# A ring of six raw weight units in the expert passes, and a router in another order with eight gather banks

## Chip, cores and metric
One core of one Trainium2 chip runs the whole program. The metric is device time in microseconds, the median of the runs.

## What is computed
Two layers over 256 tokens of width 1024. In each: a mixing block (RMSNorm, one combined projection, four mixers, gated branch products, an output projection), then a mixture of experts with a two-level choice:

```python
h = rmsnorm(x, norm2_g[l])
g_logits = t @ w_group + b_group              # 4 groups, the best one is taken
e_in = expert logits (t @ w_expert + b_expert) of that group   # 4 experts, the best 2
hid = silu(t @ w_e_gate) * (t @ w_e_up)        # experts 1024 -> 256
out = sum over the 2 experts of weight * (hid @ w_e_down)      # 256 -> 1024
x = x + out
```

## The kernel before
**Weights.** All large products are made of float32r pieces: a number is split into hi and lo, and each product is three matmuls (hi hi, hi lo, lo hi; lines 1309 to 1311). Weights come from HBM in units of up to 128 x 2048 float32 (1 MB), each by two DMAs that the SyncE queue issues in the order of use (`load`). A unit lands in a raw slot; ScalarE copies it to `w_hi` (`hi`, L500), VectorE makes `w_lo` by a subtraction (`lo`, L777). Raw slots and split slots are rings of four: a load into a slot waits until `lo` of the unit four before it is done; `hi` waits until TensorE has used the unit four before.

**Stages of a layer.** The mixing block takes 36 units. The experts are worked by passes: the router sorts tokens by group, and a pass takes 128 tokens of one group through its four experts, 12 units: eight `gate_up` units (two to an expert, k tiles 0 to 3 and 4 to 7, 12 matmuls of 512 columns each) and four `down` units. There is a pass for each group and one more where a group has over 128 tokens; layer 0 has four passes, layer 1 five. After a pass its rows go back to their tokens by `scatter`.

**The router** stands between the output projection and the first pass; nothing but the loads of the next units can run beside it. t is the half of 128 tokens. Each engine has its order written by hand:
- TensorE: the last matmuls of the projection, with the transposes of x (`turn`, L1582), the logits (`logits`, L1589), the rank of each token in its group (`rank`) and the gather products (`gather`, L1608) set between them. `gather(t, k)` multiplies k tile k of x by a 0/1 matrix `sel`, two matmuls of 512 columns, so that tokens stand sorted by group in PSUM. There are 16 for each t; seven k tiles have banks of their own, the eighth reuses the first's.
- VectorE: residual sums (`add_mid`, L1083), `lo` of the next units, the lo part of x for the gather (`rows_lo`, L1097), then chains of small dependent steps of some 0.2 us: `choose_group` (from L1103), `place`, `select` (L1118, writes `sel`), the choice of experts and their weights.
- ScalarE: squares for the norm, `rows_hi`, `hi`, then for each k tile a scaled copy of the sorted tokens from PSUM to `xg` (L693); from `xg` it makes `g_hi` of the first pass (`pass_tokens`, L506), and VectorE `g_lo` (`pass_low`, L783).

`combine_weights` (from L1664) carries each token's expert weights to the sorted order; VectorE reads the result (from L1200, five steps and a copy), then `lo(3)`, `hidden(0)` (L1231: silu times up, times the weight), `pass_table` (nine small steps), `lo(4)`, `hidden_lo(0)` (L1237). TensorE's first pass goes `gate_up(0, 0)`, `combine_weights`, `gate_up(0, 1)`, `gate_up(1, 0)`, `hidden_tp(0)` (L1707, needs `hidden(0)`), `gate_up(1, 1)`, `down(0)` (needs `hidden_lo(0)`).

Of the kernel before, what the change touches and what calls it, by code (L numbers as in the profile page):

```python
# [22 lines left out]
F32 = mybir.dt.float32  # L23
# [6 lines left out]
P = 128  # L30
# [3 lines left out]
RAW = 4  # L34
PART = 4
# [4 lines left out]
def trunk(nc, x_in, positions, norm1_g, w_in, sgu_ln_g, sgu_ln_b, sgu_w, sgu_b, q_norm_g, k_norm_g, sinks,  # L40
# [34 lines left out]
    assert all(n % r == 0 for n in (NA, NM) for r in (RAW, PART))  # L75
# [9 lines left out]
    class At:  # L85
# [11 lines left out]
        def slot(self, n, ring):  # L97
            return n % ring

        def landed(self, n):  # L100
            layers = self.l + 1 if self.moe else self.l
            return 16 * DMAS * (layers * (NA // RAW) + self.passes * (NM // RAW) + n // RAW + 1)

    with ExitStack() as ctx:
        def sb(name, shape, dt=F32):
            return ctx.enter_context(nc.sbuf_tensor(name, shape, dt))

# [3 lines left out]

        raw = sb("raw", [P, RAW, UNIT])
        w_hi = sb("w_hi", [P, PART, UNIT], F32R)
# [9 lines left out]
        u_t = sb("u_t", [P, CT * SEQ])  # L123
        v_n = sb("v_n", [P, T, MIX])
        p_t = sb("p_t", [P, 12, P])
        c_gate = sb("c_gate", [P, CT, SEQ])
        c_b = sb("c_b", [P, CT, SEQ])
# [10 lines left out]
        sgw_t = sb("sgw_t", [P, GS, P])  # L138
# [66 lines left out]
        xt_hi = a_hi[:, :].rearrange("p (k t s) -> p t k s", t=T, k=KT)  # L205
        xt_lo = a_lo[:, :].rearrange("p (k t s) -> p t k s", t=T, k=KT)
# [4 lines left out]
        xg = flat_g[:, 0:4096].rearrange("p (k s) -> p k s", k=KT)  # L211
        sq_dump = flat_g[:, 4096:6144].rearrange("p (t d) -> p t d", t=T)
# [29 lines left out]
        GT_BANKS = (2, 6, 7, 3, 0, 4, 5, 2)  # L242
        small_bank = 1
# [6 lines left out]
        landed = [sem(f"landed{i}") for i in range(RAW)]  # L250
# [48 lines left out]
        def _(sp):  # L299
# [32 lines left out]
            def load(at, n, kind, i, h, l, e=None, table=False):  # L332
                slot = at.slot(n, RAW)
                sp.wait_ge(split_done, at.ring(n))
                if table:
                    sp.wait_ge(S("tab_ready"), l + 1)
                dst = raw[:, slot, :]
# [44 lines left out]
            for l in range(DEPTH):  # L382
# [4 lines left out]
                with sp.Fori(0, NG - 1) as g:  # L387
                    at = At(l, before + g, True)
                    for n, (kind, i, h) in enumerate(units_m):
                        load(at, n, kind, i, h, l, g * EPG + i, table=n == NM - 1)  # L390
# [10 lines left out]
                if l < DEPTH - 1:  # L401
# [3 lines left out]
                    sp.wait_ge(S("gp_hi"), 2 * (before + l) + 2)  # L405
# [86 lines left out]
        def _(act):  # L492
            a = nc.scalar

            def hi(at, n):
                slot = at.slot(n, RAW)
# [3 lines left out]
                a.activation(w_hi[:, at.slot(n, PART), 0:w], raw[:, slot, 0:w], ACT.Copy).then_inc(hi_done, 1)  # L500
# [21 lines left out]
            for l in range(DEPTH):  # L522
# [144 lines left out]
                def rows_hi(t):  # L667
                    a.activation(xt_hi[:, t, :, :], x[:, t, :].rearrange("q (p c) -> q c p", c=KT),
                                 ACT.Copy).then_inc(S("xt_hi_done"), 1)
# [1106 lines left out]
```

## Time and profile before
| | us |
|---|---|
| median of 3 runs | 818.88 |
| the runs | 818.88, 815.38, 821.76 |
| the profiled execution, and its span | 823.82, 822.1 |
| TensorE busy in the span | 795.6 |
| VectorE, ScalarE busy | 658.4, 505.5 |

TensorE's busy time is made of modelled, overlapping records, so it says only that few gaps are long. Starts of successive matmuls tell more than their durations.

### The profile page before, as it was taken

How to read it: one execution, taken by the hardware profiler on the slowest of the kernel's cores; microseconds unless marked ns; L12 is line 12 of the kernel's file. 1: busy time of each engine (PE TensorE's matmuls, PEld its weight loads, DVE VectorE, ACT ScalarE, POOL GpSimd, SP SyncE). 2: the span in 40 equal slices, each digit the busy share in tenths (PEclk: the TensorE clock that was granted, in tenths of full speed). 3: DMA queues.
4: the chain of work that ended last, by engine and by line, in shares of the span. 5: the costliest groups of instructions: out<-in, count | busy, mean ns of one | idle time of the engine just before them, and what ended most of it. 6: DMA issues, size and time to landing. Idle time of an engine off the chain costs nothing. (4 is left out here: it accounts for less than half of the span.)

```text
span 822.1 us, 13258 instructions
## 1 busy us (share of the span) xinstructions
PE 795.6 (97%) x4850; PEld 703.2 (86%) x4850; DVE 658.4 (80%) x859; ACT 505.5 (61%) x573; POOL 21.7 (3%) x37
## 2 busy tenths in 40 slices
PE   8999999999999999998999999999999999999996
PEld 8899999998777788787899999999877777777875
DVE  6868996497678999898676899559758998888987
ACT  7535555653666877776644456564547677777763
POOL 4110000000000000000010000000000000000000
PEclk9999999999899999999999999999978999999998
DMA  8776353376218898998754625337422989999894
GB/s 290 260 253 208 135 169 108 103 247 213 104 48 324 315 371 338 340 333 268 252 175 156 238 103 180 103 128 259 152 102 89 347 327 350 337 353 341 316 341 162
DMA packets 80840, 189.88 MB, mean 231 GB/s; under 512 B 12534, under 2 KB 24472, under 8 KB 80792
## 3 DMA queue, kind: packets, MB, share of 16 engines
q1 hardware_dynamic: 80792, 189.23, 65.3%
q8 instruction: 32, 0.52, 0.3%
q14 instruction: 16, 0.13, 0.0%
HBM read 188.15 MB, written 1.05 MB: 230 GB/s over the span
## 5 line engine op out<-in xcount | busy, mean ns | idle before, releaser
L777 DVE TENSOR_TENSOR w_lo<-raw,w_hi 128x2048 fp32r<-128x2048 f32 (+1 forms) x182 | 400.2, 2215 | 74.2 <-ACT w_hi L500 73.6
L500 ACT ACTIVATE w_hi<-raw 128x2048 fp32r<-128x2048 f32 (+1 forms) x182 | 336.9, 1859 | 192.9 <-PE bank L1311 133.6
L1309 PE MATMUL bank<-a_hi,w_hi 128*128 128x256 f32 x688 | 197.2, 287 | 0.6 <-DVE a_lo L842 0.6
L1310 PE MATMUL bank<-a_hi,w_lo 128*128 128x256 f32 x688 | 195.9, 285 | 0.0
L1311 PE MATMUL bank<-a_lo,w_hi 128*128 128x256 f32 x688 | 195.9, 285 | 0.0
L1309 PE MATMUL bank<-w_hi,y_lo 128*128 128x512 f32 x432 | 172.9, 400 | 9.1 <-DVE y_lo L1237 6.0
L1311 PE MATMUL bank<-w_lo,y_lo 128*128 128x512 f32 x432 | 168.8, 391 | 0.0
L1309 PEld LDWEIGHTS bank<-a_hi,w_hi 128*128 128x128 f32 x688 | 133.3, 194 | 1.7 <-issue 1.6
L1310 PEld LDWEIGHTS bank<-a_hi,w_lo 128*128 128x128 f32 x688 | 133.4, 194 | 0.1
L1311 PEld LDWEIGHTS bank<-a_lo,w_hi 128*128 128x128 f32 x688 | 133.3, 194 | 0.0
L1310 PE MATMUL bank<-w_hi,y_hi 128*128 128x512 f32 x288 | 112.5, 391 | 0.0
L1309 PEld LDWEIGHTS bank<-w_hi,y_lo 128*128 128x128 f32 x432 | 81.1, 188 | 33.3 <-issue 9.1
L1311 PEld LDWEIGHTS bank<-w_lo,y_lo 128*128 128x128 f32 x432 | 81.1, 188 | 17.4
L1310 PEld LDWEIGHTS bank<-w_hi,y_hi 128*128 128x128 f32 x288 | 54.2, 188 | 10.2
L1310 PE MATMUL bank<-w_hi,y_lo 128*128 128x512 f32 x144 | 56.1, 390 | 0.0
L959 DVE SCALAR_TENSOR_TENSOR d_acc<-dpad,pcols,d_acc 128x256 f32<-128x256 f32 x120 | 48.5, 477 | 0.0
L1309 PE MATMUL bank<-w_hi,a_hi 128*128 128x512 f32 (+1 forms) x112 | 43.7, 390 | 0.0
L1310 PE MATMUL bank<-w_hi,a_lo 128*128 128x512 f32 (+1 forms) x112 | 43.3, 387 | 0.0
L1311 PE MATMUL bank<-w_lo,a_hi 128*128 128x512 f32 (+1 forms) x112 | 43.2, 386 | 0.0
L1309 PE MATMUL bank<-y_hi,w_hi 128*128 128x256 f32 x128 | 36.2, 283 | 0.0
L1310 PE MATMUL bank<-y_hi,w_lo 128*128 128x256 f32 x128 | 36.2, 283 | 0.0
L1311 PE MATMUL bank<-y_lo,w_hi 128*128 128x256 f32 x128 | 36.2, 283 | 0.0
(304 smaller groups left out, 900.0 us busy)
## 6 DMA issues: line engine op xcount, KB each, us to landing
raw<-in_w_e_gate SPq DMA_DIRECT2D x72, 512.0 KB, 4.4
raw<-in_w_e_up SPq DMA_DIRECT2D x72, 512.0 KB, 5.9
raw<-in_w_e_down SPq DMA_DIRECT2D x72, 512.0 KB, 5.4
raw<-in_w_gate SPq DMA_DIRECT2D x56, 512.0 KB, 4.5
raw<-in_w_in SPq DMA_DIRECT2D x38, 512.0 KB, 6.5
raw<-in_w_branch SPq DMA_DIRECT2D x16, 512.0 KB, 4.5
raw<-in_w_o SPq DMA_DIRECT2D x16, 512.0 KB, 4.6
raw<-in_w_gate SPq DMA_DIRECT2D x16, 256.0 KB, 2.7
```

The source lines that it names most:

```text
L500: a.activation(w_hi[:, at.slot(n, PART), 0:w], raw[:, slot, 0:w], ACT.Copy).then_inc(hi_done, 1)
L777: v.tensor_tensor(w_lo[:, part, 0:w], raw[:, slot, 0:w], w_hi[:, part, 0:w].bitcast(F32), ALU.subtract).then_inc(split_done, 1)
L959: last = v.scalar_tensor_tensor(out=d_acc[:, c, :], in0=src, scalar=w, in1=d_acc[:, c, :], op0=ALU.mult, op1=ALU.add)
L1309: mm(ps, a2[0], b2[0], start=first, stop=False, skip_group_check=shared)
L1310: mm(ps, a2[1], b2[0], start=False, stop=False, skip_group_check=shared)
L1311: return mm(ps, a2[0], b2[1], start=False, stop=last, skip_group_check=shared)
```

## The change
Two things are changed together. **The ring.** In the expert passes the raw slots are a ring of six. Slots 4 and 5 lie in a new buffer `mid`, which in the mixing block holds six of its tiles (they had buffers of their own). Units 4 and 5 of a first pass wait for the end of the mixers (`y_lo_done`) in place of `lo`; later units wait for `lo` of the unit six before. The first pass's loads stand outside SyncE's loop.

**The router.** `rows_lo(0)` comes ahead of `add_mid(1, 0)` and `lo(1)` behind `choose_group(0)`; `rows_hi(1)` and `rows_lo(1)` are halves. The eighth gather tile takes bank 1, where the small results stand; so the count is read before `select(1)`, and `combine_weights` writes bank 2. `g_hi` and `g_lo` of the first pass are made from PSUM, in eight pieces each (`first_tokens`, `first_low`); the copies to `xg` (`keep_tokens`) come after. `hi(3)` moves into the router. On TensorE `combine_weights` stands behind `gate_up(0, 1)`. The silu table is loaded between `keep_tokens` of tiles 3 and 4.

```diff
+        def free(self, n, first):
+            deep = RAW if self.moe and first and n < RAW or not self.moe and (n >= RAW or self.l == 0) else RAW_M
+            return self.unit(n) + 1 + RAW - deep
...
+        def raw_at(slot):
+            return raw[:, slot, :] if slot < RAW else mid[:, (slot - RAW) * UNIT:(slot - RAW + 1) * UNIT]
...
         raw = sb("raw", [P, RAW, UNIT])
+        mid = sb("mid", [P, (RAW_M - RAW) * UNIT])
...
+        u_t = mid[:, 0:512]
...
+        sgw_t = mid[:, 3584:4096].rearrange("p (g s) -> p g s", g=GS)
...
-        GT_BANKS = (2, 6, 7, 3, 0, 4, 5, 2)
-        small_bank = 1
+        GT_BANKS = (6, 7, 2, 3, 0, 4, 5, 1)
+        small_bank, cw_bank = 1, 2
...
+                if first and RAW <= n < RAW_M:
+                    sp.wait_ge(S("y_lo_done"), 4 * (l + 1))
+                else:
+                    sp.wait_ge(split_done, at.free(n, first))
...
+                at = At(l, before, True)
+                for n, (kind, i, h) in enumerate(units_m):
+                    load(at, n, kind, i, h, l, i, table=n == NM - 1, first=True)
+                with sp.Fori(1, NG - 1) as g:
...
@@ -675,30 +695,46 @@
                 square_mid(0, 0)
                 square_mid(0, 1)
-                rows_hi(0)
+                rows_hi(0, 0, P)
                 turned(0)
                 hi(at, 1)
                 square_mid(1, 0)
+                rows_hi(1, 0, P // 2)
                 turned(1)
                 a.activation(warm[:, 0:1], ones[0:1, 0:1], ACT.Exp)
                 square_mid(1, 1)
-                rows_hi(1)
+                rows_hi(1, P // 2, P)
                 hi(at, 2)
+                hi(at, 3)
                 act.wait_ge(S("gd_done"), l + 1)
                 a.activation(r4[:, 2, :, :].rearrange("p t g -> p (t g)"), r4[:, 1, :, :].rearrange("p t g -> p (t g)"),
                              ACT.Exp).then_inc(S("ge_done"), 1)
                 act.wait_ge(par_r, 16 * 5 * (l + 1))
-                for k in range(KT):
+
+                def first_tokens(k):
                     act.wait_ge(S("g_tp"), KT * l + k + 1)
+                    a.activation(g_hi[:, k, :], bank[GT_BANKS[k]][:, 0:P], ACT.Identity,
+                                 scale=g2[:, k:k + 1]).then_inc(S("g0_hi"), 1)
+
+                def keep_tokens(k):
+                    act.wait_ge(S("g0_lo"), KT * l + k + 1)
                     a.activation(xg[:, k, :], bank[GT_BANKS[k]][:, :], ACT.Identity,
                                  scale=g2[:, k:k + 1]).then_inc(S("g_act"), 1)
-                    if k == 4:
-                        act.wait_ge(S("g_act"), KT * l + 4)
-                        pass_tokens(0, 0)
-                        act.wait_ge(S("dm_done"), l + 1)
-                        a.activation(r1[:, 8, :], r1[:, 7, :], ACT.Exp).then_inc(S("x2_done"), 1)
-                act.wait_ge(S("g_act"), KT * (l + 1))
-                pass_tokens(1, 0)
+
+                for k in range(4):
+                    first_tokens(k)
+                keep_tokens(0)
+                first_tokens(4)
+                keep_tokens(1)
+                for k in range(5, KT):
+                    first_tokens(k)
+                act.wait_ge(S("dm_done"), l + 1)
+                a.activation(r1[:, 8, :], r1[:, 7, :], ACT.Exp).then_inc(S("x2_done"), 1)
+                keep_tokens(2)
+                keep_tokens(3)
+                a.activation(warm[:, 0:1], ones[0:1, 0:1], ACT.Silu)
+                for k in range(4, KT):
+                    keep_tokens(k)
...
-                    a.activation(warm[:, 0:1], ones[0:1, 0:1], ACT.Silu)
-                    hi(at, 3)
+                    if not first:
...
                 lo(at_m, 0)
                 mean_square(0)
                 turned(0)
-                lo(at_m, 1)
+                rows_lo(0, 0, 0, P)
                 dve.wait_ge(S("o_part"), l + 1)
                 add_mid(1, 0)
-                rows_lo(0)
                 choose_group(0)
                 step.do(v.memset(ov[:, 0:1], 0.0))
+                lo(at_m, 1)
                 used(NA - 1)
                 add_mid(1, 1)
                 place(0)
...
                 turned(1)
-                rows_lo(1)
+                rows_lo(1, 1, 0, P // 2)
...
                 v.tensor_tensor(r4[:, 1], lg[:, :, 0:NG], b4(gm), ALU.subtract).then_inc(S("gd_done"), 1)
                 step.do(v.tensor_tensor(lq[:, :, :], widx[:, 3:5, :], bc(goh[:, 1, :], [P, 2, NG], 1), ALU.mult))
                 step.do(v.tensor_reduce(r1[:, 12, :], lq[:, :, :], AX, ALU.add))
+                rows_lo(2, 1, P // 2, P)
                 place(1)
                 step.do(v.tensor_scalar(ov[:, 1:2], rk[:, 1:2], r1[:, 12, 0:1], None, ALU.is_ge))
                 step.do(v.tensor_scalar(r1[:, 16, 1:2], rk[:, 1:2], -2.0, r1[:, 12, 1:2], ALU.mult, ALU.add))
                 step.do(v.scalar_tensor_tensor(out=pos[:, 1:2], in0=r1[:, 16, 1:2], scalar=ov[:, 1:2], in1=rk[:, 1:2],
                                                op0=ALU.mult, op1=ALU.add))
+                step.do(v.tensor_copy(cnt[:, 0, :], small_ps[:, COUNT:COUNT + NG]))
                 select(1)
-                for t in range(T):
-                    v.tensor_scalar(diag[:, t, :], ident[:, :], pos[:, t:t + 1], None, ALU.mult).then_inc(S("diag_done"), 1)
...
+                def first_low(k):
+                    dve.wait_ge(S("g0_hi"), KT * l + k + 1)
+                    v.scalar_tensor_tensor(out=g_lo[:, k, :], in0=bank[GT_BANKS[k]][:, 0:P], scalar=g2[:, k:k + 1],
+                                           in1=g_hi[:, k, :].bitcast(F32), op0=ALU.mult,
+                                           op1=ALU.subtract).then_inc(S("g0_lo"), 1)
+
...
                 first_max(oh1, ein, r1[:, 3], 4)
+                first_low(0)
+                first_low(1)
                 step.do(v.scalar_tensor_tensor(out=e2, in0=oh1, scalar=NEG, in1=ein, op0=ALU.mult, op1=ALU.add))
                 first_max(oh2, e2, r1[:, 5], 6)
                 v.tensor_tensor(r1[:, 7, :], r1[:, 5, :], r1[:, 3, :], ALU.subtract).then_inc(S("dm_done"), 1)
+                first_low(2)
+                first_low(3)
                 dve.wait_ge(S("ge_done"), l + 1)
                 step.do(v.tensor_reduce(r1[:, 9, :], r4[:, 2], AX, ALU.add))
                 step.do(v.reciprocal(r1[:, 10, :], r1[:, 9, :]))
-                step.do(v.tensor_copy(cnt[:, 0, :], small_ps[:, COUNT:COUNT + NG]))
+                for k in range(4, KT):
+                    first_low(k)
                 step.do(v.tensor_scalar(cnt[:, 1, :], cnt[:, 0, :], float(P), None, ALU.is_gt))
-                pass_low(before + l, 0, 0)
+                for t in range(T):
+                    v.tensor_scalar(diag[:, t, :], ident[:, :], pos[:, t:t + 1], None, ALU.mult).then_inc(S("diag_done"), 1)
...
-                pass_low(before + l, 1, 0)
                 lo(at, 2)
                 dve.wait_ge(S("cw_done"), l + 1)
...
                     if k == KT - 1:
-                        pe.wait_ge(S("g_act"), KT * l + 1)
                         gather(0, k)
                     gather(1, k).then_inc(S("g_tp"), 1)
                 def combine_weights():
                     pe.wait_ge(S("diag_done"), T * (l + 1))
                     pe.wait_ge(S("cm_lo_done"), 2 * (l + 1))
-                    mm(bank[small_bank][:, POSB:POSB + SEQ], ones[:, :], diag[:, :, :].rearrange("p t s -> p (t s)"),
+                    pe.wait_ge(S("g_act"), KT * l + 3)
+                    mm(bank[cw_bank][:, POSB:POSB + SEQ], ones[:, :], diag[:, :, :].rearrange("p t s -> p (t s)"),
...
                 def expert_pass(at, PP, first):
                     def gate_up(e, h, n):
-                        if e == 0:
-                            pe.wait_ge(S("gp_lo"), 2 * (PP + l) + h + 1)
+                        if first and e == 0:
+                            pe.wait_ge(S("g0_lo"), KT * l + 4 * h + 4)
+                        elif e == 0:
+                            pe.wait_ge(S("gp_lo"), 2 * (PP - 1) + h + 1)
+                        if first and h == 0 and e < 2:
+                            pe.wait_ge(S("g_act"), KT * l + e + 1)
...
                         pe.wait_ge(S("hd_lo_done"), EPG * PP + e + 1)
+                        if first and e == 0:
+                            pe.wait_ge(S("g_act"), KT * l + 7)
...
                     gate_up(0, 0, 0)
+                    gate_up(0, 1, 1)
                     if first:
                         combine_weights()
-                    gate_up(0, 1, 1)
                     gate_up(1, 0, 2)
                     hidden_tp(0)
                     gate_up(1, 1, 3)
```

## Rows read from the trace of the kernel before

**Rows 1.** First line of the page: the span of the profiled execution.
```profile
span 822.1 us, 13258 instructions
```
**Rows 2.** Busy time by stage; last three columns: TensorE clock (1.00 = 2.4 GHz), DMA share, GB/s.
```profile
216.10:220.60 4.50, 4.50 (x16) 3.27 (x13) 2.40 (x7) 2.35 (x5) 0.00 (x0) 0.62 0.63 233
...
618.10:624.80 6.70, 6.50 (x19) 4.85 (x18) 3.98 (x22) 4.78 (x9) 0.00 (x0) 0.66 0.00 0
...
700.00:736.00 36.00, 35.81 (x159) 28.55 (x158) 32.25 (x26) 27.29 (x26) 0.00 (x0) 1.00 0.95 346
```
**Rows 3.** Timeline of TensorE, layer 0's router: start, duration, instruction, idle before it and releaser.
```profile
215.67 0.66 PE L1582 MATMUL bank<-ident,x 128*128 128x128 f32 x4 [1.44 <-DVE x L1083]
...
218.07 0.63 PE L1311 MATMUL bank<-w_lo,a_hi 128*128 128x512 f32 x1
218.49 0.63 PE L1309 MATMUL bank<-w_hi,a_hi 128*128 128x512 f32 x1
...
231.71 0.80 PE L1608 MATMUL bank<-y_hi,a_hi 128*128 128x512 f32 x1
...
234.22 0.39 PE L1608 MATMUL bank<-y_hi,a_lo 128*128 128x512 f32 x1
234.45 0.39 PE L1608 MATMUL bank<-y_hi,a_hi 128*128 128x512 f32 x1
...
237.53 0.50 PE L1309 MATMUL bank<-w_hi,y_lo 128*128 128x512 f32 x1 [0.66 <-DVE y_hi L783]
...
240.63 1.14 PE L1668 MATMUL bank<-cmr,y_hi 128*128 128x18 f32 x8
...
247.20 0.38 PE L1707 MATMUL bank<-ident,gates 128*128 128x128 f32 x2
...
251.06 0.47 PE L1309 MATMUL bank<-w_hi,y_lo 128*128 128x512 f32 x1 [0.73 <-DVE y_lo L1237]
```
**Rows 4.** The same of VectorE, layer 0's router and first pass.
```profile
212.72 2.29 DVE L777 TENSOR_TENSOR w_lo<-raw,w_hi 128x2048 fp32r<-128x2048 f32 x1 [2.19 <-ACT w_hi L500]
214.93 0.68 DVE L1083 TENSOR_TENSOR x<-bank,x 128x512 f32<-128x512 f32 x1
215.53 2.05 DVE L1097 TENSOR_TENSOR a_lo<-x,a_hi 128x1024 fp32r<-128x1024 f32 x1
...
227.26 0.24 DVE L1103 SCALAR_TENSOR_TENSOR d_acc<-bank,rs,rb 128x20 f32<-128x20 f32 x1 [1.01 <-PE bank L1589]
...
231.17 0.48 DVE L1118 TENSOR_SCALAR y_hi<-iota,d_acc 128x512 fp32r<-128x512 f32 x1
...
242.56 0.22 DVE L1200 COPY d_acc<-bank 128x72 f32<-128x72 f32 x1
...
246.28 0.47 DVE L1231 SCALAR_TENSOR_TENSOR gates<-gates,d_acc,bank 128x256 f32<-128x256 f32 x1
...
250.49 0.42 DVE L1237 TENSOR_TENSOR y_lo<-bank,y_lo 128x256 fp32r<-128x256 f32 x1
```
**Rows 5.** The same of ScalarE, layer 0's router.
```profile
233.03 3.13 ACT L693 ACTIVATE gates<-bank,g 128x512 f32<-128x512 f32 x5 [4.18 <-PE bank L1608]
...
239.19 1.28 ACT L719 ACT_TABLE_LOAD   x1
```
**Rows 6.** Timeline of TensorE, layer 1: the same place as the last of group 3.
```profile
638.32 0.47 PE L1309 MATMUL bank<-w_hi,y_lo 128*128 128x512 f32 x1 [0.69 <-DVE y_lo L1237]
```
**Rows 7.** Waits of TensorE, 238 to 392, then 640 to 792: us in total, times, longest.
```profile
PE bank L1309 <- DVE y_lo L1237: 2.0, 3, 0.8
...
PE bank L1309 <- DVE y_lo L1237: 1.9, 3, 1.4
```
**Rows 8.** Timelines of TensorE and ScalarE, layer 1, fourth and fifth pass.
```profile
757.59 0.47 PE L1309 MATMUL bank<-w_hi,y_lo 128*128 128x512 f32 x1 [1.39 <-DVE y_lo L1237]
...
795.15 0.47 PE L1309 MATMUL bank<-w_hi,y_lo 128*128 128x512 f32 x1 [1.42 <-DVE y_lo L1237]
...
754.80 1.91 ACT L500 ACTIVATE w_hi<-raw 128x2048 fp32r<-128x2048 f32 x1 [2.16 <-DMA raw<-in_w_e_up]
```

More of the change, by code:

```diff
@@ L74, in trunk @@
     NA, NM = len(units_a), len(units_m)
-    assert all(n % r == 0 for n in (NA, NM) for r in (RAW, PART))
+    assert all(n % r == 0 for n, r in ((NA, RAW), (NA, PART), (NM, RAW_M), (NM, PART)))
     G0, O0 = 10, 32
@@ L95, in ring, with raw, part @@
             return self.unit(n) + 1
-        def slot(self, n, ring):
-            return n % ring
+        def raw(self, n):
+            return n % (RAW_M if self.moe else RAW)
+        def part(self, n):
+            return n % PART
+        def free(self, n, first):
+            deep = RAW if self.moe and first and n < RAW or not self.moe and (n >= RAW or self.l == 0) else RAW_M
+            return self.unit(n) + 1 + RAW - deep
         def landed(self, n):
-            layers = self.l + 1 if self.moe else self.l
-            return 16 * DMAS * (layers * (NA // RAW) + self.passes * (NM // RAW) + n // RAW + 1)
+            layers = (self.l + 1 if self.raw(n) < RAW else 0) if self.moe else self.l
+            ring = RAW_M if self.moe else RAW
+            return 16 * DMAS * (layers * (NA // RAW) + self.passes * (NM // RAW_M) + n // ring + 1)
     with ExitStack() as ctx:
@@ L211, in trunk @@
         xg = flat_g[:, 0:4096].rearrange("p (k s) -> p k s", k=KT)
+        xt_hi = [a_hi[:, :].rearrange("p (k t s) -> p t k s", t=T, k=KT)[:, 0],
+                 y_lo[:, 0:2, :].rearrange("p a s -> p (a s)").rearrange("p (k s) -> p k s", k=KT)]
+        xt_lo = [a_lo[:, :].rearrange("p (k t s) -> p t k s", t=T, k=KT)[:, t] for t in range(T)]
         sq_dump = flat_g[:, 4096:6144].rearrange("p (t d) -> p t d", t=T)
@@ L241, in trunk @@
         X_BANKS = ((6, 7), (4, 5))
-        GT_BANKS = (2, 6, 7, 3, 0, 4, 5, 2)
-        small_bank = 1
+        GT_BANKS = (6, 7, 2, 3, 0, 4, 5, 1)
+        small_bank, cw_bank = 1, 2
         LG, RANK, COUNT, POSB = (0, 32), (64, 68), 72, 256
         bank = [ctx.enter_context(nc.psum_tensor(f"bank{i}", [P, 512], F32)) for i in range(8)]
-        landed = [sem(f"landed{i}") for i in range(RAW)]
+        landed = [sem(f"landed{i}") for i in range(RAW_M)]
         hi_done = sem("hi_done")
@@ L330, in router_parameters, with load @@
                 sp.dma_start(g2[:, :], norm2_g[l].rearrange("(p c) -> p c", c=KT)).then_inc(par_r, 16)
-            def load(at, n, kind, i, h, l, e=None, table=False):
-                slot = at.slot(n, RAW)
-                sp.wait_ge(split_done, at.ring(n))
+            def load(at, n, kind, i, h, l, e=None, table=False, first=False):
+                slot = at.raw(n)
+                if first and RAW <= n < RAW_M:
+                    sp.wait_ge(S("y_lo_done"), 4 * (l + 1))
+                else:
+                    sp.wait_ge(split_done, at.free(n, first))
                 if table:
                     sp.wait_ge(S("tab_ready"), l + 1)
-                dst = raw[:, slot, :]
+                dst = raw_at(slot)
                 for j in range(DMAS):
@@ L404, in _ @@
                     mixer_parameters(nxt)
-                    sp.wait_ge(S("gp_hi"), 2 * (before + l) + 2)
+                    sp.wait_ge(S("g_act"), KT * (l + 1))
                     router_parameters(nxt)
@@ L1258, in expert_pass @@
                     hidden(3)
-                    pass_low(PP + l + 1, 0, tile_next)
-                    pass_low(PP + l + 1, 1, tile_next)
+                    pass_low(PP, 0, tile_next)
+                    pass_low(PP, 1, tile_next)
                     hidden_lo(3)
@@ L1313, in parts @@
             def parts(at, n, shape, **kw):
-                s = at.slot(n, PART)
+                s = at.part(n)
                 return [w[:, s, :].rearrange(shape, **kw) for w in (w_hi, w_lo)]
```

49 lines of the change are left out of this document (23 added, 26 removed).

## Prediction
> **What bounds the kernel now.** I read the stages first: the busy time in stretches, with TensorE's clock [rows 2]. A stretch of 36 us in the passes, almost one pass, has TensorE busy 35.8 us at 2.4 GHz, with the DMA engines 0.95 busy at 346 GB/s. So the passes are TensorE's, and DMA is close behind. The routers look otherwise: two stretches there stand at 0.62 and 0.66 of full clock, which is the half level (1.2 GHz) for two thirds of them and more, and VectorE and ScalarE have long idle parts. Next the timelines of one router engine by engine [rows 3 to 6]: who released the first instruction after each gap. Last the waits of TensorE in the passes and the chain behind the longest [rows 7, 8].
>
> A 512-column matmul starts 0.23 us after the one before at full clock (234.22, 234.45) and 0.43 us at half (218.07, 218.49) [rows 3]. A unit of 12 matmuls and its switch takes 2.8 us at full clock, `combine_weights` 1.2 us.
>
> **The router, step by step**, in layer 0's times. "Full" below means that the clock never drops.
>
> *First gap.* TensorE ends `logits(0)` at about 214.1 and waits for `add_mid(1, 0)` until 215.67 [rows 3]: VectorE stood idle 2.19 us for `hi(1)`, then did `lo(1)` (2.2 us) ahead of the sum [rows 4]. The change puts `rows_lo(0)` (2.05 us) into that idle time, so the sum is done at 213.3 and the transposes start at 214.1: 1.6 us won. `choose_group(0)` follows the logits at 214.3 and takes 1.1 us, `lo(1)` ends at 217.7. The 12 matmuls of the projection that follow now need 3.1 us with the transposes, so `add_mid(1, 1)` waits 0.2 us for `lo(1)` and ends at 218.4, where it ended at 221.5. But 1.5 us of these 3.1 are won only if the clock stays up: before, eight of these matmuls ran at half, behind the gap and the small logits (first stretch of [rows 2]). The edit takes the gap out, not the logits, so I call this part likely, not sure.
>
> *Second half.* `select(0)` and the transposes let `logits(1, 0)` start at 219.2; then 6 gather matmuls (1.4 us full, 2.6 half) and `logits(1, 1)` (1.0): `choose_group(1)` starts at 222.6 full, 223.8 half, against 227.26 [rows 4]. It waited for TensorE there, so splitting `rows_lo(1)` alone wins nothing before it; the second half (1.05 us) lies in the idle time while TensorE does `rank(1)` (1.5 us). The count's copy (0.2 us) is on the path. `select(1)` ends at 227.1 full; it ended at 231.65 [rows 4].
>
> *Gather and first tokens.* The last 18 gather matmuls take 4.2 us full; they took 5.2 (231.71 to 236.9) [rows 3], 6.2 in layer 1 (two thirds of that stretch at half, 618.1 to 624.8 in [rows 2]), and would take 7.7 all at half. In their shadow run `first_tokens` and `first_low`. No row has these shapes. Between 0.24 us (128x20 from PSUM) and 0.47 (128x256) [rows 4] I take 0.35, 0.27 from start to start; for ScalarE the same, below 0.63 of a 512-column copy [rows 5]. VectorE's six to eight small steps between them take 1.2 to 1.4 us; tiles 0 to 3 are ready at 231.0, TensorE is free at 231.3, so nothing waits; with either end (0.2 or 0.5 each) the first `gate_up` moves by 0 to 0.7 us. The wait of 0.66 us for `pass_low` goes [rows 3]. The first pass starts at 231.4 full, against 237.53. `keep_tokens` and the silu table (a load of 1.3 us in the same engine's queue [rows 5]) end near 237 to 239, with `hi(4)` behind them by 241; `lo(4)` needs that only at 244. Free.
>
> The same eight pieces are where a rule speaks against the change. The Trainium skill ("VectorE: DVE Perf Modes", the section on the errata) says each VectorE or ScalarE instruction pays a fixed latency, 120 cycles of 0.96 GHz from PSUM and 58 from SBUF, and advises tiles of 512 elements or more. By its figures eight pieces are an estimated 2.1 us against 1.2 us for the two of before, 0.9 us more in each layer. The rows stand a little above it (0.47 us for 256 columns, where it gives 0.39); the pieces lie under the gather in the sum above, and would add 1.8 us to the kernel if they were on the path.
>
> *What gives it back.* `combine_weights` ends 6.8 us after the first pass starts (2.8 + 2.8 + 1.2) and not 4.2. Behind its end VectorE has a chain that is not shortened: five small steps and the copy of positions (1.5 us), `lo(3)` (2.2), `hidden(0)` (0.4), `pass_table` (1.6), `lo(4)` (2.2), `hidden_lo(0)` (0.4), from 242.56 to 250.9, and `down(0)` starts at 251.06 at its end [rows 3, 4]: 8.5 us. Before, `lo(2)` held its start back by 0.8 us (results at 241.8, read at 242.56); now `lo(2)` is done in time. So `down(0)` starts 15.3 us after the first pass, where it was 13.5: 1.8 of the 6.1 us are lost again. I expect TensorE to wait about 1.5 us at `hidden_tp(0)` (before it came there at 247.20, after `hidden(0)`'s 246.7 [rows 3, 4]) and 1.2 us at `down(0)` (0.73 before).
>
> *Sum of a router.* Full: `down(0)` at 246.7, 4.35 us earlier in layer 0. Layer 1's clock had been worse: its place is 638.32 [rows 6], 253.1 when shifted by the 385.2 us between the layers, so 6.4 us. But low activity remains (small matmuls, 1 to 2 us of waits at `rank(1)` and `select(1)`), so I take half clock for the first six gathers (+1.2) and for a part of the last 18 (+0.8 in layer 0, +1.4 in layer 1): `down(0)` at 248.7 and 249.3, that is 2.4 + 3.8 = 6.2 us. If the projection's matmuls still drop too, 1.6 less in each: 3.0 us.
>
> **The ring.** In the passes after `down(0)`, the gaps that name `hidden_lo` (L1237) have DMA at their root: ScalarE stood 2.16 us for an up-weight, its `hi` then came before `hidden`, and `down` waited 1.39 us [rows 8]. Such gaps are 1.9 us in layer 1 from 640 to 792 [rows 7], with one of 1.42 after it [rows 8], and 1.3 us in layer 0 (2.0 without the 0.73 at the first `down(0)`) [rows 3, 7]: 4.6 us. The few gaps at a pass's start for `lo(2)` come from ScalarE's own order and stay. Two more slots let each load start two units earlier and have eight units landed or under way at the router's end in place of six. Capacity is there: a pass needs 12.6 MB in 36.6 us, 344 GB/s, while 346 at a share of 0.95 makes 364 [rows 2]. Bounds: 0 if the DMA engines are at their limit, 4.6 if every gap goes; I take 3.9, as a 6% margin is thin. Loads placed in SyncE's queue: units 4 and 5 wait for `y_lo_done`, long past when their turn comes, so nothing is held behind them. The silu preload leaves five or seven later passes: under 0.2 us each, on ScalarE, not counted.
>
> **From the profiled execution to the median.** 6.2 + 3.9 = 10.1 us from 823.82 is 813.7. That execution (span 822.1 [rows 1], 1.7 us outside it) is 4.9 us above the median, and what runs differ by is what this change works on (half clock, DMA waits), so the median has less of it to lose. From 818.88 all 10.1 us give 808.8. I take the middle: **811.3 us**, 7.6 us (0.9%) less.
>
> **Rivals.** About 1% is what a measurement of this kernel can tell from no change, 8.2 us.
> - *The clock stays up*: both routers full and every DMA gap gone: 4.35 + 6.4 + 4.6 = 15.4 us, 808.4 from the profiled execution and 803.5 from the median, some 805. For: the first gap was the same in both layers and goes. Against: `rank`, logits and waits stay. Chance 0.2.
> - *The ring brings nothing* because the DMA engines, 0.95 busy, are the limit and a deeper ring only queues: 6.2 us, 817.6 from the profiled execution and 812.7 from the median, so 815.2. Against: 364 GB/s above. The case that the projection still runs at half lies beside it (3.0 + 3.9 = 6.9 us, 814.5 in the same way). Chance together 0.3.
> - *Slower: the postponed `combine_weights` at half clock.* Its place is `hidden_tp(0)` and `down(0)` of the first pass. It decides from the point where the first pass starts later than 235.8, since 235.8 + 6.8 is the 242.6 at which VectorE read the results before. With every router matmul at half the first pass starts at 238.1 (231.4 + 1.6 + 1.2 + 0.4 + 3.5), and `down(0)` at 253.4, 2.3 us late in layer 0 and 0.3 in layer 1; the two new waits then sit in a stretch with 1.2 us of small matmuls, and each stretch of eight matmuls at half there costs 1.6 us, one or two to a layer: 2.6 + 3.2 to 6.4 us, 825 to 828. The Trainium skill ("TensorE: Matmul & The Clock Gate", on oscillation in real kernels) says that idle pauses between bursts of matmuls put the array back to half rate, which would put this rival at its upper end, 828. The rows show such a drop behind the first gap, and none behind the gaps of 0.66 and 0.73 us. Chance 0.06.
> - *My forecast*: 0.44, own range 808 to 815.
>
> Range 803.5 to 819: it leaves out the slower rival and the tails. Faster by over 1% (below 810.7): the first rival and half of my own case, 0.42. Within 1%: 0.52. Slower: 0.06.
>
> **What would show it.** Right: no gap ahead of the second transposes; the first pass about 4 to 6 us earlier against the projection; `down(0)` 15.3 us after it, with gaps near 1.5 and 1.2 us at `hidden_tp(0)` and `down(0)`; ScalarE's waits for DMA in the passes a small part of before. Wrong: half clock over the last gather in both layers; gaps for `hidden_lo` still there in the last passes; the loads still at 340 GB/s with ScalarE waiting.

## Result and the profile after

The changed kernel takes 810.75 us, median of 4 runs (806.85 to 811.95), against 820.17 of the kernel before (815.38 to 821.76): ratio 0.988, 95% interval 0.984 to 0.992. A second set on another occasion gave 808.22 against 819.33, ratio 0.987 (0.983 to 0.990). The span of the profiled execution fell from 822.1 to 810.0 us.

The timeline of TensorE, layer 0's router, in the changed kernel (start, duration, instruction, and in brackets the idle time before it and who ended it):

```profile
211.00 1.85 PE L1636 MATMUL bank<-wrs,xn 128*128 128x20 f32 x16
212.70 0.64 PE L1629 MATMUL bank<-ident,x 128*128 128x128 f32 x4
...
215.71 0.39 PE L1358 MATMUL bank<-w_lo,a_hi 128*128 128x512 f32 x1
...
217.04 0.66 PE L1629 MATMUL bank<-ident,x 128*128 128x128 f32 x4 [0.32 <-DVE x L1119]
...
225.78 0.80 PE L1655 MATMUL bank<-y_hi,y_lo 128*128 128x512 f32 x1 [0.89 <-DVE y_hi L1154]
...
231.50 0.59 PE L1655 MATMUL bank<-y_hi,a_lo 128*128 128x512 f32 x1
231.93 0.40 PE L1655 MATMUL bank<-y_hi,a_hi 128*128 128x512 f32 x1
...
232.85 0.39 PE L1356 MATMUL bank<-w_hi,y_lo 128*128 128x512 f32 x1
...
238.54 1.14 PE L1715 MATMUL bank<-cmr,y_hi 128*128 128x18 f32 x8
...
243.97 0.44 PE L1758 MATMUL bank<-ident,gates 128*128 128x128 f32 x2 [1.43 <-DVE gates L1278]
...
248.18 0.47 PE L1356 MATMUL bank<-w_hi,y_lo 128*128 128x512 f32 x1 [1.00 <-DVE w_lo L813]
```

Against [rows 3]: the gap of 1.44 us ahead of the second transposes is gone (212.70 follows the logits at once), and the projection's last matmuls run at full clock. The first pass (232.85) has no wait ahead of it. Three waits are new or larger, all for VectorE: 0.89 us for `select(1)` ahead of the last gathers, 1.43 at `hidden_tp(0)` and 1.00 at `down(0)`. And the last gathers, from 225.78, are at half clock to 231.9. The stretches say the same; the columns are those of [rows 2]:

```profile
225.80:231.90 6.10, 6.10 (x14) 4.77 (x15) 4.11 (x22) 3.19 (x8) 0.00 (x0) 0.50 0.00 1
232.80:248.20 15.40, 12.97 (x62) 10.26 (x61) 13.19 (x40) 12.64 (x17) 0.00 (x0) 1.00 0.43 137
```

VectorE in the same router and the start of the first pass, changed kernel:

```profile
209.07 2.16 DVE L1133 TENSOR_TENSOR a_lo<-x,a_hi 128x1024 fp32r<-128x1024 f32 x1
211.19 0.69 DVE L1119 TENSOR_TENSOR x<-bank,x 128x512 f32<-128x512 f32 x1
...
225.24 0.49 DVE L1154 TENSOR_SCALAR y_hi<-iota,d_acc 128x512 fp32r<-128x512 f32 x1
...
229.84 0.60 DVE L1203 SCALAR_TENSOR_TENSOR y_hi<-bank,g,y_lo 128x128 fp32r<-128x128 f32 x2
...
233.46 0.35 DVE L1203 SCALAR_TENSOR_TENSOR y_hi<-bank,g,y_lo 128x128 fp32r<-128x128 f32 x1 [0.57 <-ACT y_lo L716]
...
236.59 0.17 DVE L1244 TENSOR_TENSOR cmr<-d_acc,cmr 128x16 fp32r<-128x16 f32 x1
236.68 2.28 DVE L813 TENSOR_TENSOR w_lo<-raw,w_hi 128x2048 fp32r<-128x2048 f32 x1
239.72 0.23 DVE L1247 COPY d_acc<-bank 128x72 f32<-128x72 f32 x1 [0.76 <-PE bank L1715]
...
243.44 0.47 DVE L1278 SCALAR_TENSOR_TENSOR gates<-gates,d_acc,bank 128x256 f32<-128x256 f32 x1
```

`rows_lo(0)` now fills the hole of [rows 4]; a `first_low` piece takes 0.35 us; the results are read at 239.72, right after they come, where [rows 4] had them read late behind `lo(2)`.

In the passes the gaps for `hidden_lo` are nearly gone. The waits of TensorE in layer 1's passes (us in total, times, longest), first the kernel before, then the changed one:

```profile
PE bank L1309 <- DVE y_lo L1237: 3.3, 4, 1.4
PE bank L1309 <- DVE w_lo L777: 0.9, 3, 0.6
...
PE bank L1356 <- DVE w_lo L813: 0.6, 1, 0.6
PE bank L1356 <- DVE y_lo L1284: 0.3, 1, 0.3
```

and of ScalarE in layer 0's passes, before and changed; the copies of weights now wait for TensorE, and no line names a DMA:

```profile
ACT w_hi L500 <- DMA raw<-in_w_e_up: 13.2, 12, 2.3
ACT w_hi L500 <- DMA raw<-in_w_e_down: 8.5, 12, 1.9
...
ACT w_hi L520 <- PE bank L1358: 4.9, 8, 1.8
ACT w_hi L520 <- issue: 2.1, 3, 1.1
```

So these copies waited 21.7 us for loads before, and no longer do. The 12.1 us by which the span fell divide as follows (from the start of the first residual sum to the first pass, on to the start of `down(0)`, then to the start of the last scatter):

| stretch, us | before, layer 0 and 1 | changed, layer 0 and 1 | won |
|---|---|---|---|
| first sum to first pass | 31.29, 33.39 | 27.99, 28.06 | 3.30 + 5.33 |
| first pass to `down(0)` | 13.53, 13.47 | 15.33, 15.37 | -1.80 - 1.90 |
| `down(0)` to last scatter | 137.15, 175.70 | 135.70, 171.34 | 1.45 + 4.36 |
| all else | | | 1.4 |

The last 1.4 us lie ahead of the first router, nearly all in the start of the kernel, which the change does not touch. So the changed parts won 10.7 us: the routers 4.9, the passes 5.8. That is one execution against one. The router of before stands in eight readings (two layers in each of `before`, `ring_only`, `ring_again` and `half_loads`, below): `down(0)` comes 44.0 to 46.9 us after the first sum, mean 44.8. The new router stands in six (this profile, its repetition, `router_only`): 40.6 to 45.3, mean 42.8. By these the two routers win 4.0 us.

### The profile page after: what moved, and what is told of

The parts are those of the page before. It is cut to its first block and busy times, and to the rows that moved or that the text cites. A ratio compares the mean times of both kernels' runs of the same rounds, so it can differ in the third digit from the quotient of the medians.

```text
span 810.0 us, 13178 instructions
## 1 busy us (share of the span) xinstructions
PE 784.6 (97%) x4850; PEld 696.2 (86%) x4850; DVE 661.7 (82%) x873; ACT 507.3 (63%) x580; POOL 21.6 (3%) x37
## 5 line engine op out<-in xcount | busy, mean ns | idle before, releaser
L813 DVE TENSOR_TENSOR w_lo<-raw,w_hi 128x2048 fp32r<-128x2048 f32 (+1 forms) x146 | 318.2, 2198 | 66.7 <-ACT w_hi L520 66.2
L520 ACT ACTIVATE w_hi<-raw 128x2048 fp32r<-128x2048 f32 (+1 forms) x146 | 267.7, 1843 | 141.9 <-PE bank L1358 134.9
L813 DVE TENSOR_TENSOR w_lo<-mid,w_hi 128x2048 fp32r<-128x2048 f32 x36 | 82.2, 2282 | 0.0
L520 ACT ACTIVATE w_hi<-mid 128x2048 fp32r<-128x2048 f32 x36 | 68.7, 1909 | 4.0 <-PE bank L1358 4.0
L746 ACT ACTIVATE gates<-bank,d_acc 128x256 f32<-128x256 f32 x36 | 17.0, 471 | 32.9 <-PE bank L1358 31.6
```

Of the source, the lines that this page charges most:

```text
L520: a.activation(w_hi[:, at.part(n), 0:w], raw_at(slot)[:, 0:w], ACT.Copy).then_inc(hi_done, 1)
L746: a.activation(sil[:, e % 2, :], bank[6 + e % 2][:, 0:F], ACT.Silu, scale=rslot[:, 0:1] if first else rcur).then_inc(S("sil_done"), 1)
L813: v.tensor_tensor(w_lo[:, part, 0:w], raw_at(slot)[:, 0:w], w_hi[:, part, 0:w].bitcast(F32), ALU.subtract).then_inc(split_done, 1)
```

## Experiments

The runs of one kernel differ by up to 16 us, so few of the ratios can settle a question of 2 us. Three further readings help. One is the table above for each kernel's profile. The second uses the mean granted clock that each run reports: over all 166 runs of the kernels in the table below, one straight line for each kernel, with one slope in common, fits to 1.4 us; the slope is 5.5 us for each 0.01 of clock. "At equal clock" below is the line's value at 0.985, with an error of about 0.2 us for the kernel before (66 runs), 0.35 for the ring alone (20) and 0.45 to 0.6 for the others; a difference to the kernel before has 0.4 to 0.6, one to the changed kernel 0.6 to 0.75. A time at equal clock leaves out what a kernel wins by having fewer matmuls at half clock.

```
kernel            runs  mean clock  at 0.985   | down(0) after first sum (half)  passes
before              66    0.983       817.7    | 44.8 (20)   46.9 (30)    137.2  175.7
changed             10    0.989       810.8    | 43.3 (14)   43.4 (14)    135.7  171.3
  its second profile                           | 42.8 (13)   41.4 (6)     135.7  171.4
ring_only/_again    20    0.980       812.3    | 44.0 (12)   44.7 (20)    135.4  171.1
router_only         10    0.988       817.6    | 45.3 (21)   40.6 (0)     139.2  175.6
half_loads          10    0.982       812.7    | 44.9 (19)   44.7 (20)    135.4  171.1
first_gap           10    0.986       814.6    | 41.7 (12)   41.9 (12)    138.1  173.4
combine_back        10    0.986       809.6    | 39.6 (0)    41.1 (6)     135.7  171.1
late_table           6    0.989       809.2    | 43.5 (21)   40.1 (6)     136.3  171.7
filler               6    0.991       811.1    | 40.5 (0)    40.6 (0)     135.7  171.4
late_filler          6    0.987       809.7    | 38.7 (0)    38.8 (0)     136.2  171.7
earlier_weights      6    0.989       807.4    | 39.0 (0)    40.6 (14)    135.8  171.1
earlier_filler       6    0.986       808.6    | 41.6 (14)   39.1 (0)     135.8  171.1
```

"Half" counts the router's 512-column matmuls at half clock in the profiled execution, to about one; in `earlier_filler`, layer 0, it includes the four of the filler. Layer 0 stands left, layer 1 right.

A third reading follows from the counts. A matmul at half clock starts its successor 0.20 us later (0.43 in place of 0.23), so 0.2 us times the count, taken off, gives an estimate of the router with none at half: 40.9 us for the router of before (mean of eight, 40.5 to 41.6), 40.5 for the new one (six, 40.2 to 41.1), 39.3 for `first_gap` and 39.7 for `combine_back` (two each).

**The ring alone** (the change's lines for `mid`, `free`, `landed` and the loads, with all orders of before).

```diff
+RAW_M = 6
...
+                slot = at.raw(n)
...
+                    sp.wait_ge(split_done, at.free(n, first))
```

> The ring of six with the router of before. If the two parts add (theory): the passes lose their DMA waits as in the changed kernel, so 136 us from the first down(0) to the last scatter in layer 0 and 171.5 in layer 1 (137.2 and 175.7 before), ratio 0.993 to before, and the router keeps its 1.4 us gap. If the DMA engines are the limit (rival): gaps for hidden_lo stay, passes 137 and 175, ratio 1.00.

Measured: 815.69 us, ratio 0.998 (0.993 to 1.002). The passes took 135.4 and 171.1 us, as expected; the router kept its gap. The ratio missed the 0.993 that I expected; the runs had a lower clock (mean 0.979), and at equal clock this kernel is 5.4 us below the one before, 0.7%. Waits of TensorE in layer 1's passes:

```profile
PE bank L1328 <- DVE w_lo L796: 0.9, 3, 0.6
PE bank L1328 <- DVE y_lo L1256: 0.3, 1, 0.3
```

It was run again for the clock:

> The ring of six with the router of before, again: its first runs had a mean clock of 0.979 where the kernel before has 0.983. Theory (that was chance, the ring does nothing to the clock): mean clock 0.982 to 0.983 and ratio 0.993. Rival (with no waits for DMA something else lowers the clock): again 0.979 and ratio 0.997.

Measured: 813.10 us, ratio 0.994 (0.991 to 0.998); mean clock 0.981, between the theory and the rival. Both sets taken together, 8 of 20 runs stood at 0.975 or below, of `half_loads` 3 of 10, of the kernel before 7 of 66. So it is not settled whether the old router behind passes without late loads gets a low clock more often, or whether this was chance. At equal clock the ring wins 5.4 us. The passes of the ring of four differ more between executions than those of six: both layers together 312.9 us in `before`, 314.8 in `router_only`, 311.5 in `first_gap`, against 306.6 to 307.1 wherever six slots are used without later edits.

**The router alone**, with the ring of four.

```diff
-RAW_M = 6
+RAW_M = 4
...
-        mid = sb("mid", [P, (RAW_M - RAW) * UNIT])
+        mid = sb("mid", [P, 2 * UNIT])
```

> The changed kernel with RAW_M = 4, so the router's new order with the ring of four. Theory: down(0) stands where the changed kernel has it (some 43.3 us after the first residual sum), ScalarE waits for DMA in the passes again by about 20 us a layer, passes 137 and 175 us as before; ratio 0.994. Rival (the router's win needs the two units loaded ahead): down(0) as in the changed kernel but more lost behind it, the passes longer than before by 1 to 2 us in each layer, ratio 0.998 or above.

Measured: 815.75 us, ratio 0.998 (0.995 to 1.001); 0.1 us less than before at equal clock, so its win is that its runs stand at 0.988 in place of 0.983. The ratio is the rival's (0.998), not the 0.994 expected, and the ratios of the two parts alone do not add up to that of both (0.988). At equal clock 5.4 and 0.1 make 5.5 of the 6.9 us; the rest is within what these errors and the spread of the passes with four slots allow. In layer 1 of the profiled execution no router matmul was at half, and `down(0)` came 40.6 us after the first sum, the 40.5 that the prediction's sum gave for a router at full clock (246.7 less 206.2). Layer 0 had 21 at half, and 45.3. ScalarE waited 25 us for loads in layer 0's passes, which were 2.1 us longer than before, as the rival had it. But layer 1's passes, behind a router 6.3 us quicker, took 175.6 us, as before; so it is not shown that a quicker router makes the two units loaded ahead worth more.

```profile
ACT w_hi L520 <- DMA raw<-in_w_e_up: 16.9, 13, 3.4
ACT w_hi L520 <- DMA raw<-in_w_e_down: 8.4, 13, 1.4
```

**Half loads**: the kernel before with half of each expert weight transfer left out, so its output is not the reference's.

```diff
-                        d = dst[:, 1024 * j:1024 * j + 1024].rearrange("p (c f) -> p c f", c=4)
+                        d = dst[:, 1024 * j:1024 * j + 512].rearrange("p (c f) -> p c f", c=2)
```

> The kernel before with each expert weight DMA halved: it loads half of each unit of the passes, and the other half holds what was there, so the expert weights are wrong in part. It bounds what any ring can win. Theory: all gaps of TensorE that come from a late load go, the passes take 135.7 and 171.4 us as with the ring of six, ratio 0.993. Rival (the ring of six still loses time to DMA): passes shorter than the ring's by over 1 us a layer, ratio 0.990 or below.

Measured: 813.80 us, ratio 0.994 (0.990 to 0.999); passes 135.4 and 171.1 us. This is the ring's result to 0.1 us, and TensorE's waits in layer 1's passes are the same two lines:

```profile
PE bank L1309 <- DVE w_lo L777: 0.9, 3, 0.6
PE bank L1309 <- DVE y_lo L1237: 0.3, 1, 0.3
```

So six slots take away all that the loads cost the passes: 1.7 + 4.6 = 6.3 us in the profiles, 5.0 (this kernel) and 5.4 (the ring) at equal clock. The DMA engines were not the limit: with half the bytes the passes are no shorter than with six slots.

**The first gap alone**: the kernel before with one reorder on VectorE.

```diff
                 turned(0)
-                lo(at_m, 1)
+                rows_lo(0)
                 dve.wait_ge(S("o_part"), l + 1)
                 add_mid(1, 0)
-                rows_lo(0)
                 choose_group(0)
                 step.do(v.memset(ov[:, 0:1], 0.0))
+                lo(at_m, 1)
```

> The kernel before with one edit: rows_lo(0) ahead of add_mid(1, 0) and lo(1) behind choose_group(0). Theory: TensorE's gap of 1.4 us ahead of the second transposes goes, and with it the drop of the clock over the projection's last matmuls (8 at half before), so their 12 take 3.1 us in place of 4.9; add_mid(1, 1) 3.1 us earlier after the first residual sum, mean granted clock of the runs 0.002 higher; ratio 0.996. Rival (the logits alone bring the clock down): the gap goes, but eight of these matmuls stay at half; ratio 0.999.

Measured: 813.86 us, ratio 0.994 (0.991 to 0.997). The transposes follow the logits, and all 12 matmuls behind them are at full clock:

```profile
213.18 1.85 PE L1589 MATMUL bank<-wrs,xn 128*128 128x20 f32 x16
214.88 0.64 PE L1582 MATMUL bank<-ident,x 128*128 128x128 f32 x4
215.27 0.47 PE L1309 MATMUL bank<-w_hi,a_hi 128*128 128x512 f32 x1
216.05 0.40 PE L1309 MATMUL bank<-w_hi,a_hi 128*128 128x512 f32 x1
```

The other profiles say the same. In all eight routers that have the gap of 1.43 or 1.44 us, six to eight of these 12 are at half; in the other twenty, which have the logits and no gap, none is. So the gap, together with the logits, brought the clock down there, not the logits alone. `down(0)` comes 3.1 us earlier in layer 0 and 5.0 in layer 1. At equal clock this one edit wins 3.1 us, and its runs stand at 0.986. The whole new router with the same ring wins 0.1 us at equal clock at 0.988. The counts say why. With none at half, `first_gap` is 1.6 us quicker than the router of before in each layer (40.9 to 39.3), and the whole new router 0.4 (to 40.5): its postponed `combine_weights` gives back 1.8 us behind the start of the first pass, and its other edits win 0.6 ahead of it, the wait of 0.63 us for `pass_low` that `first_gap` still has before its first pass and no new router has. The matmuls at half number 20 of 67 on average in the router of before, 12 in `first_gap` and 11 in the new router, so the gap accounts for most of these too.

**`combine_weights` back** ahead of `gate_up(0, 1)`, in the changed kernel.

```diff
-                    gate_up(0, 1, 1)
                     if first:
                         combine_weights()
+                    gate_up(0, 1, 1)
```

> The changed kernel with combine_weights before gate_up(0, 1) again. By my account of VectorE's chain, TensorE now waits 1.2 us at combine_weights for the last of the chosen weights (VectorE ends them at 236.8, gate_up(0, 0) ends at 235.6), the results are read after lo(2) at 238.9 in place of 239.7, and down(0) comes 0.8 us earlier in each layer; no gap at hidden_tp(0); ratio to before 0.986. Rival (the postponement costs its full 2.8 us a layer): 5 us less than the changed kernel, ratio 0.981.

Measured: 808.88 us, ratio 0.991 (0.987 to 0.995), where 0.986 was expected: its runs had a clock of 0.986, those of the changed kernel 0.989. At equal clock it is 1.2 us less than the changed kernel, with an error of 0.6; 1.6 expected. TensorE waits at the place and for the time expected, `hidden_tp(0)` has no gap, and `down(0)` comes 14.5 us after the first pass in both layers, 0.8 earlier than 15.3:

```profile
235.36 0.67 PE L1711 MATMUL bank<-gates,ones 128*128 128x256 f32 x2 [1.15 <-issue]
```

"Issue" here is the last of the weights on VectorE, `cmr` (L1244), done at 235.26. The rival (5 us) falls.

**VectorE's chain cut**, in the changed kernel.

```diff
                 lo(at, 2)
+                lo(at, 3)
                 dve.wait_ge(S("cw_done"), l + 1)
...
-                    lo(at, 3)
+                    if not first:
+                        lo(at, 3)
                     hidden(0)
-                    if first:
-                        pass_table()
                     lo(at, 4)
                     hidden_lo(0)
                     lo(at, 5)
                     hidden(1)
+                    if first:
+                        pass_table()
+                        v.tensor_copy(posb[:, :], bank[cw_bank][:, POSB:POSB + SEQ]).then_inc(S("posb_read"), 1)
```

> The changed kernel with VectorE's chain behind combine_weights cut: lo(3) ahead of the read of the weights, pass_table and the copy of positions after hidden(1). Theory (this chain sets down(0) in the first pass): hidden(0) ends 0.9 us earlier, down(0) starts 2.0 us earlier in each layer, at 13.3 us after the first pass starts in place of 15.3; ratio to the changed kernel 0.995. Rival (the work only moves): later gaps of the first pass grow by as much, passes 137.5 us in layer 0, no difference.

Measured: 805.92 us, ratio 0.984 (0.982 to 0.987). `down(0)` starts 13.5 us after the first pass in both layers (43.48 less 29.99, 40.08 less 26.56), 1.8 us better than 15.3; then `lo(6)` is late by 0.44 and 0.41 us, and the passes are 0.6 and 0.4 us longer:

```profile
246.62 0.44 PE L1760 MATMUL bank<-ident,gates 128*128 128x128 f32 x2 [0.78 <-DVE gates L1276]
255.90 0.50 PE L1358 MATMUL bank<-w_hi,y_lo 128*128 128x512 f32 x1 [0.44 <-DVE w_lo L813]
```

Between a quarter and a third of the win moves on, the rest stays. At equal clock it is 1.6 us less than the changed kernel, with an error of 0.7.

**A filler for the clock**, in the changed kernel: matmuls whose result is overwritten.

```diff
-                for k in range(5, 7):
-                    gather(0, k)
+                gather(0, 5)
+                for _ in range(4):
+                    mm(bank[GT_BANKS[6]][:, :], xt_hi[0][:, 5, :], sel[:, 0, :], start=True, stop=True)
+                gather(0, 6)
```

> The changed kernel with four more matmuls of 512 columns, whose result is thrown away, in the gap of 0.9 us ahead of the last gathers. Theory (TensorE's low activity there brings the clock down to 1.2 GHz over the last 14 gather matmuls, 2.8 us in each layer): none or fewer of them at half, the first pass starts up to 2.8 us earlier, ratio to the changed kernel 0.995. Rival (the clock's fall does not depend on this gap, but on the small matmuls ahead): the same count at half as without, no gain, at worst 0.1 us lost a layer.

> The changed kernel once more, timed on the same chip as the three below. Theory: ratio to before 0.988 to 0.991; down(0) at 40.6 us after the first residual sum if no gather matmul is at half clock, 43.4 if fourteen are. Rival (the 0.9878 was partly chance, since the ring and the router alone gave 0.9975 and 0.9979): 0.993 to 0.996.

> Both edits together. If they add: 2.0 and up to 2.8 us in each layer, 7 us less than the changed kernel on average, ratio to before 0.981. If the filler does nothing: as late_table.

Measured: the changed kernel again 808.22 us, ratio 0.987 (0.983 to 0.990), so the first result was no chance. Its second profile had 13 and 6 router matmuls at half and `down(0)` at 42.8 and 41.4 us, in line with the 40.6 for none and 43.4 for fourteen that I expected. With the filler 806.15, 0.987 (0.983 to 0.992); with both edits 808.66, 0.988 (0.985 to 0.991). In the filler's profiled execution the last gathers ran at full clock, and the first pass began 25.1 us after the first sum where it was 28.0:

```profile
224.04 1.08 PE L1700 MATMUL bank<-y_hi,a_hi 128*128 128x512 f32 x4
...
225.55 0.50 PE L1655 MATMUL bank<-y_hi,y_lo 128*128 128x512 f32 x1
225.88 0.40 PE L1655 MATMUL bank<-y_hi,a_lo 128*128 128x512 f32 x1
```

But the filler's six runs had clocks from 0.980 to 0.997, those of both edits 0.984 to 0.994, and the changed kernel without it 0.983 to 0.995. Kernels without the filler also had routers with none at half (router_only layer 1, combine_back layer 0). In the profiled executions five of six routers with the filler had none at half, of the new router without it three of twelve; but the mean clock is 0.988 over 18 runs with the filler and 0.989 over 22 without. So one execution at full clock shows what a better clock is worth, not that the filler brought it; over the runs it made no difference that can be told.

**The weights earlier**: the chain cut, `combine_weights` back, and VectorE's steps for the weights set between `first_low(4)` and `first_low(7)`.

```diff
+                first_low(4)
                 step.do(v.tensor_scalar(cnt[:, 1, :], cnt[:, 0, :], float(P), None, ALU.is_gt))
...
+                first_low(5)
                 dve.wait_ge(S("x2_done"), l + 1)
...
+                first_low(6)
...
+                first_low(7)
```

> The changed kernel with the steps of the expert weights set between first_low 4 to 7, where VectorE stood idle 0.2 to 0.6 us each time, combine_weights before gate_up(0, 1) again, and pass_table and the copy of positions after hidden(1). Theory: the weights are ready when gate_up(0, 0) ends, TensorE has no wait over 0.3 us from the first pass to down(0), which comes at 12.6 us after the first pass starts (15.3 in the changed kernel); 2.7 us a layer, less 0.4 for lo(6) later; ratio to the changed kernel 0.994. Rival (the clock's chance outweighs it): the profile as above, the ratio within 0.997 to 1.003.

> The same with the four matmuls of no use ahead of the last gathers. The filler took half clock off the profiled execution (0.997) but not off all runs (0.980 to 0.997). If it helps: mean clock at least 0.990 and ratio to before 0.980. If it does not: as earlier_weights, mean clock 0.988.

Measured: 804.87 us, ratio 0.981 (0.977 to 0.985), the best of all; at equal clock 3.4 us less than the changed kernel, with an error of 0.7; 4.6 expected. With the filler 808.41, ratio 0.985 (0.981 to 0.989), mean clock 0.986: no help again. `down(0)` comes 12.5 us after the first pass in layer 1, as expected, but 13.9 in layer 0, where the gathers were at full clock: TensorE then gets to `combine_weights` before the weights are ready, a wait that I had not expected:

```profile
234.02 0.67 PE L1714 MATMUL bank<-gates,ones 128*128 128x256 f32 x2 [1.16 <-issue]
```

## Why the prediction was right

The forecast was 811.3 us, measured were 810.75. The mechanism came in at each place that it named but the last gathers; that the number is so close is in part luck. The router won 1.3 us less than forecast and the ring 1.9 more, which nearly cancel, and the kernel before was measured at 820.17 in place of 818.88, so that the difference is 9.4 us and not 7.6. Point by point, times counted from the first residual sum (206.24 in layer 0 before).

- *First gap*: right in place and size. The last sum of the second half starts at 11.4 us (before at 14.5) and ends at the 12.1 that the sum gave. The part called likely, not sure, came in: the projection's last matmuls stayed at full clock in both layers, and `first_gap` shows that the reorder alone does it.
- *Second half*: `choose_group(1)` began at 16.35 us and `select(1)` ended at 20.9, both the full-clock figures to 0.1 us.
- *Last gathers*: the router's mis-sized term, and the prediction had named half clock there in both layers as a sign of being wrong. I took 5.0 and 5.6 us; 14 of 18 were at half in both layers, and they took 7.1. In the second profile of the same kernel 3 of 18 were, and they took 4.9 and 5.0, so the size goes by the execution. In exchange the first six gathers, for which I had taken 1.2 us of half clock, ran full. The first pass began at 28.0 us where I had 27.2 (layer 0) and 27.8 (layer 1). The router in all: 4.9 us won, 6.2 forecast.
- *First tokens*: 0.35 us each, as taken between the rows' ends, and hidden. Cutting them into small pieces cost nothing on the path, since TensorE's gathers set the time: TensorE has no wait ahead of the first pass, and where no gather was at half (`router_only`, layer 1) that pass began at 25.2 us, the 25.2 of the sum (231.4 less 206.2). So the 1.8 us that the rule against small pieces would have cost did not come. Of the figures that the prediction quotes with that rule, 120 and 58 cycles, both are VectorE's alone; ScalarE's pieces took 0.37 us each here.
- *What gives it back*: 15.33 and 15.37 us from the first pass to `down(0)`, 15.3 predicted; waits of 1.43 and 1.00 us, 1.5 and 1.2 predicted. `combine_back` and `late_table` show the cause: with the chain cut the time is 13.5, with the step put back it is 14.5, so `down(0)` is 0.8 us earlier, not 2.8.
- *Ring*: the other mis-sized term, 5.8 us won, 3.9 forecast, above my bound of 4.6. The bound was the sum of the gaps listed; `half_loads` put the cost of late loads at 6.3. Held against `ring_only` matmul by matmul, layer 1 loses most of its time at the starts of `down` units. The three listed gaps there (0.25, 1.39 and 1.42 us idle) put the matmuls behind them off by 3.8 us, 0.7 more than their idle time, and delays of up to 0.3 us that are not listed made most of the rest of 4.6. That the ring takes all of it settles what I had held back for the DMA engines' thin margin: nothing was lost to it.
- *From execution to median*: the profiled execution before stood high partly by its clock (0.976, where the mean over 66 runs is 0.983). The middle way, a choice without a working, came out right: 10.7 us won in the changed parts of the profiles, 6.9 at equal clock and some 3 from the higher clock in the runs.
- *The slower rival* asked for the first pass to begin later than 29.6 us after the first sum; in `router_only`, layer 0, it did (30.0), and `down(0)` came at 45.3, 0.5 us later than before. So half clock over the router's matmuls can bring the pass that late, but in none of the 28 first passes profiled was a matmul at half between its start and the end of `down(0)`. (The middle of this prediction's 808.4 and 803.5 for the first rival is 806.0, not 805; no chance or bound hangs on it.)

What stays open: whether the new router's other edits do anything to the count at half; the parts were not run one by one. That the passes in `router_only` were 2.0 us longer than before, and 3.3 longer than in `first_gap`, hides part of their win at equal clock.

## What to carry to other kernels

Before a step is moved later on the busy engine, follow the chain that starts at its result on the other engines: here 8.5 us of VectorE's work hung on `combine_weights`, and that chain, not TensorE, set when the pass could go on. When an engine has a hole and later a rush, one swap that fills the hole can be most of what a large reorder wins; try it alone. To bound what buffers can win, shrink the transfers and compare that kernel's stretch with the one of before: the listed gaps understate it.

## What was not expected of the hardware

The spread between runs of one kernel, 810 to 826 us before, goes with the granted clock: 5.5 us for each 0.01. One slope fits all kernels here (lines of their own have 3 to 8, most within their errors) except `first_gap`, whose ten runs show 0.8 with an error of 1.4. Most of the half clock lies in the routers, some at layer 1's last scatter and in the mixing block (0.97 over 440 to 500 us, before and changed), and which matmuls it covers changes from one execution to the next: 0, 6, 13, 14 or 21 in the same new router. Once down, it stayed down over 14 matmuls back to back (225.78 to 231.9, clock 0.50) with TensorE busy throughout. The wait ahead of these gathers does not decide it: in eight routers it is the same, 0.88 to 0.91 us, and behind it 0, 0, 0, 6, 6, 14, 14 and 14 of the 18 last gathers were at half. What does decide is open.
